# Gathering token rows in quarter pieces and transposing them on VectorE in a mixture-of-experts layer

## What is computed

```
idx, w = route(h2, w_router, bias)          # top 8 of 64 experts for every token
for each expert e:
    rows  = tokens that chose e
    y     = (silu(h2[rows] @ w_gate[e]) * (h2[rows] @ w_up[e])) @ w_down[e]
    acc[rows] += y * w[rows, e]
```

## Time and profile before

| | us |
|---|---|
| median of 3 runs (988.42 to 990.00) | 989.62 |
| span of the profiled execution | 986.4 |
| PE busy | 932.8 |
| DVE busy | 360.1 |
| ACT busy | 162.6 |
| POOL busy | 226.8 |
| data moved | 301.04 MB, mean 305 GB/s |

### The profile page before, as it was taken

How to read it: one execution, slowest core, us unless ns; L and a number is a source line. 1 busy time by engine, 2 the same in 40 slices (tenths; PEclk the granted TensorE clock), 3 DMA queues, 4 the chain that set the end, 5 groups by cost and what they waited for, 6 DMA issues and landing times.

```text
span 986.4 us, 15652 instructions
## 1 busy us (share of the span) xinstructions
PE 932.8 (95%) x6359; PEld 483.9 (49%) x6359; DVE 360.1 (37%) x773; ACT 162.6 (16%) x304; POOL 226.8 (23%) x344
## 2 busy tenths in 40 slices
PE   6999999999999999999999999989979889897798
PEld 4678788888655533333333333344323333332344
DVE  5565673336436733333332110111101111111687
ACT  2001324210011211111111111111101102121021
POOL 4115923162100112222222222212121211201110
PEclk9999999999999999999999999999989999999899
DMA  9940005421482699999999999999999999999972
GB/s 331 331 129 1 1 1 184 158 86 63 143 317 107 223 385 386 407 418 395 411 420 407 398 422 410 408 422 415 397 422 421 421 421 419 419 401 373 380 270 85
DMA packets 83912, 301.04 MB, mean 305 GB/s; under 512 B 9299, under 2 KB 35959, under 8 KB 59648
## 3 DMA queue, kind: packets, MB, share of 16 engines
q1 hardware_dynamic: 70144, 263.19, 67.8%
q0 software_dynamic: 11920, 33.63, 8.8%
q10 hardware_dynamic: 1776, 3.21, 0.9%
HBM read 279.26 MB, written 29.36 MB: 313 GB/s over the span
## 4 chain that ended last, share of the span: by engine, by line
PE 74%; DMA 20%; SPq 2%; DVE 2%; issue 1%; ACT 1%; POOL 0%; ACTq 0%; POOLq 0%
PE ps L2223 22%; DMA ring<-in_w_exp_up 18%; PE ps L1826 12%; PE ps L2252 8%; PE ps L1976 6%; PE ps L1955 5%; PE ps L2367 4%; PE ps L1782 3%; PE ps L1759 2%; PE ps L2047 1%; PE ps L1788 1%; DMA ring<-accumulator 1%; PE ps L2232 1%; DMA accumulator<-actT,stage 1%; SPq L525 1%; PE ps L1875 1%
## 5 line engine op out<-in xcount | busy, mean ns | idle before, releaser
L2223 PE MATMUL ps<-ring,gates 128*32 128x512 f32 x2560 | 289.3, 604 | 26.1 <-DMA ring<-in_w_exp_up 25.3
L2223 PEld LDWEIGHTS ps<-ring,gates 128*32 128x32 f32 x2560 | 88.8, 111 | 218.6 <-issue 217.7
L2252 PE MATMUL ps<-ring,poolbuf 128*32 128x512 f32 x1280 | 145.6, 595 | 3.1 <-DMA ring<-in_w_exp_down 3.1
L1573 DVE COPY poolbuf<-ps 128x256 f32<-128x256 f32 x40 | 17.0, 424 | 355.4 <-PE ps L2232 355.4
L791 POOL TENSOR_TENSOR tickets<-cst 128x1 f32<-128x1 f32 x77 | 14.5, 188 | 397.1 <-ACT actT L991 391.7
L2252 PEld LDWEIGHTS ps<-ring,poolbuf 128*32 128x32 f32 x1280 | 37.9, 109 | 83.5 <-issue 81.9
L991 ACT ACTIVATE actT<-ps,qT 128x1024 f32<-128x1024 f32 x40 | 44.5, 1113 | 142.3 <-PE ps L2252 142.3
L983 ACT ACTIVATE poolbuf<-ps 128x256 f32<-128x256 f32 x40 | 15.4, 384 | 280.0 <-PE ps L2223 280.0
L1826 PE MATMUL ps<-xrow,ring 128*128 128x256 f32 x256 | 57.9, 381 | 0.1
L1976 PE MATMUL ps<-ring,gates 128*128 128x512 f32 x128 | 56.4, 594 | 0.0
L1759 PE MATMUL ps<-cst,rows 128*128 128x128 f32 x352 | 47.6, 281 | 8.3 <-DVE rows L1087 8.3
(11 more groups left out here) (294 smaller groups left out, 1062.3 us busy)
## 6 DMA issues: line engine op xcount, KB each, us to landing
ring<-in_w_exp_down SPq DMA_DIRECT2D x64, 1024.0 KB, 17.6
ring<-in_w_exp_gate SPq DMA_DIRECT2D x62, 1024.0 KB
ring<-in_w_exp_up SPq DMA_DIRECT2D x62, 1024.0 KB
ring<-accumulator SPq DMA_DIRECT2D x12, 1024.0 KB, 13.1
ring<-in_w_gate SPq DMA_DIRECT2D x8, 1024.0 KB, 13.2
ring<-in_w_in SPq DMA_DIRECT2D x5, 1024.0 KB, 12.9
xrow<-in_x SPq DMA_DIRECT2D x8, 512.0 KB, 5.1
accumulator<-ring SPq DMA_DIRECT2D x1, 4096.0 KB, 19.9
```

Of the source, the lines that this page charges most:

```text
L2223: last = mm(bank(2 + k)[part, :], hgT[k][:, q, part], pair_view(EXPERT_SLOT[js[c]])[:, q], start=(q == 0), stop=(q == KD - 1))
L2252: last = mm(bank(6 + half)[part, :], eactT[r % 2][:, q, part], w[:, q, half * 512:(half + 1) * 512], start=(q == 0), stop=(q == 1))
```

## The change

The gathered rows come as quarters. `h2_dram` is seen as 2,048 rows of 256 numbers. One step has four gathers (c = 0 to 3), each of 128 pieces of 1 KB: partition 32q + n of columns 256c to 256c + 255 receives quarter q of the row in place 32c + n. With this layout, transposing each 32x32 block by itself gives the same `hgT` as before, so one VectorE operation (`block_T`) replaces eight TensorE transposes and two copies. Step 0 alone is still gathered in whole rows and transposed on TensorE.

For the pieces, VectorE makes `quarter_at`, four index columns per step, by 16 small operations per group (`quarters_of`). GpSimd reads the indices from there, without the stage copy. Lists are made in the steps of `LIST_STEP` = 0, 1, 2, 4, 5, 7, 8, 10, 12, 13, 15, 16, 18, 20, 21, 23 for groups 0 to 15, not in steps 0 to 15. `block_T(r+1)` stands first in VectorE's step r, ahead of `act_T(r-1)`, and waits for all four pieces.

```diff
+LIST_STEP = [0] + [1 + 22 * (g - 1) // 14 for g in range(1, NGROUP)]
...
+        h2_quarters = h2_dram.rearrange("t (q d) -> (t q) d", q=STRIPS)
...
+        def quarters_gathered(r):
+            return 64 * (r // BUF + 1) - (48 if r % BUF == 0 else 0)
...
-            def stage_from(r, j):
-                pool.wait_ge(rows_listed, STEP_OF[r][0] + 1)
-                nc.gpsimd.tensor_copy(stage[:, 0, j, :], from_row[:, r:r + 1]).then_inc(staged, 1)
...
-            def gather(j):
-                pool.indirect_dma_start(hg[j], None, h2_dram,
-                                        bass.IndirectOffsetOnAxis(ap=stage[:, 0, j, :], axis=0),
-                                        bounds_check=T - 1, oob_is_err=False).then_inc(gathered[j], 16)
+            def gather(r, j):
+                for c in range(STRIPS):
+                    pool.indirect_dma_start(hg[j][:, c * 256:(c + 1) * 256], None, h2_quarters,
+                                            bass.IndirectOffsetOnAxis(ap=quarter_at[:, 4 * r + c:4 * r + c + 1], axis=0),
+                                            bounds_check=4 * T - 1, oob_is_err=False).then_inc(gathered[j], 16)
...
                 if not last:
-                    pool.wait_ge(hgT_ps, 2 * r + 2)
-                    stage_from(r + BUF, j)
+                    if r:
+                        pool.wait_ge(blocks_ready, r)
+                    else:
+                        pool.wait_ge(hgT_ps, 2)
+                    pool.wait_ge(rows_listed, STEP_OF[r + BUF][0] + 2)
...
+            def quarters_of(g):
+                n = steps_of(g)
+                r = slice(FIRST_STEP[g], FIRST_STEP[g] + n)
+                at = quarter_at[:, 4 * FIRST_STEP[g]:4 * (FIRST_STEP[g] + n)].rearrange("p (s c) -> p s c", c=STRIPS)
+                for q in range(STRIPS):
+                    for c in range(STRIPS):
+                        last = nc.vector.tensor_scalar(at[q * STRIP:(q + 1) * STRIP, :, c],
+                                                       row_of[c * STRIP:(c + 1) * STRIP, r], float(STRIPS), float(q),
+                                                       ALU.mult, ALU.add)
+                last.then_inc(rows_listed, 1)
...
+            def block_T(r):
+                j = r % BUF
+                dve.wait_ge(gathered[j], quarters_gathered(r))
+                if r >= 2:
+                    dve.wait_ge(gu_ps, STRIPS * (r - 1))
+                nc.vector.transpose(hgT[r % 2].rearrange("p k (c n) -> p k c n", c=STRIPS),
+                                    hg[j].rearrange("p (c d k) -> p k c d", c=STRIPS, k=KD)).then_inc(blocks_ready, 1)
...
             for r in range(STEPS):
...
+                if r + 1 < STEPS:
+                    block_T(r + 1)
                 if r:
                     act_T(r - 1, (r - 1) % 2)
                 act_rows(r, r % 2)
-                if r + 1 < STEPS:
-                    rows_T(r + 1, (r + 1) % 2)
-                if 1 <= r < NGROUP:
+                if r in LIST_STEP[1:]:
...
                 up(r)
                 if r:
                     acts_T(r - 1)
-                if r + 1 < STEPS:
-                    rows_T(r + 1)
-                if 1 <= r < NGROUP:
-                    lists(r)
+                if r in LIST_STEP[1:]:
+                    lists(LIST_STEP.index(r))
```

More of the change, by code:

```diff
@@ L257, in build @@
         selb = ka[:, WM:WM + NR // 2].bitcast(BF16)
+        quarter_at = ka[:, 800:800 + 4 * STEPS].bitcast(U32)
         tokc = ka[:, WM + NR // 2:WM + NR // 2 + NT * TCOL // 2].bitcast(BF16).rearrange("p (i c) -> p i c", i=NT)
@@ L815, in move @@
                 if not last:
-                    pool.wait_ge(hgT_ps, 2 * r + 2)
-                    stage_from(r + BUF, j)
+                    if r:
[3 more added lines that the diff above has]
+                    pool.wait_ge(rows_listed, STEP_OF[r + BUF][0] + 2)
                     if not first:
                         pool.wait_ge(ticket_done[0], r)
-                    pool.wait_ge(staged, 2 * r + BUF + 1)
                     ticket(0, ticket_done[0])
-                    gather(j)
+                    gather(r + BUF, j)
                 if before is not None:
@@ L827, in move @@
                     pool.wait_ge(ticket_done[1], r)
-                pool.wait_ge(staged, STEPS + r + 1 if last else 2 * r + BUF + 2)
+                pool.wait_ge(staged, r + 1)
                 pool.wait_ge(y_ready, r + 1)
@@ L834, in _ @@
             pool.wait_ge(y_first, 16)
-            for r in range(BUF):
-                stage_from(r, r)
-                pool.wait_ge(staged, r + 1)
-                gather(r)
+            gather_first()
+            pool.wait_ge(rows_listed, 2)
+            for r in range(1, BUF):
+                gather(r, r)
             for r in range(STEPS):
@@ L1009, in _ @@
             nc.scalar.activation(hgT[0][:, 0:4, :], bank(0).rearrange("p (k n) -> p k n", k=4),
-                                 ACT.Copy).then_inc(hgT_lo_ready, 1)
-            rows_hi(0, 0)
+                                 ACT.Copy).then_inc(first_T_ready, 1)
+            act.wait_ge(hgT_ps, 2)
+            nc.scalar.activation(hgT[0][:, 4:8, :], bank(1).rearrange("p (k n) -> p k n", k=4),
+                                 ACT.Copy).then_inc(first_T_ready, 1)
             shared_silu_of(1)
@@ L1454, in rows_of @@
                 link(nc.vector.tensor_scalar(tile_of, found[:, :, 1], float(T), None, ALU.add))
-                nc.vector.tensor_tensor(from_row[:, r], tile_of, found[:, :, 0], ALU.add).then_inc(rows_listed, 1)
+                if g == 0:
+                    nc.vector.tensor_tensor(from_row[:, r], tile_of, found[:, :, 0], ALU.add).then_inc(rows_listed, 1)
                 link(nc.vector.tensor_tensor(row_of[:, r], tile_of, found[:, :, 0], ALU.add))
+            def quarters_of(g):
[8 more added lines that the diff above has]
+                last.then_inc(rows_listed, 1)
             dve.wait_ge(list_ps, 1)
@@ L1606, in _ @@
                 act_rows(r, r % 2)
-                if r + 1 < STEPS:
-                    rows_T(r + 1, (r + 1) % 2)
-                if 1 <= r < NGROUP:
-                    dve.wait_ge(list_ps, r + 1)
-                    rows_of(r, found_of(r))
-                    if r == 1:
+                if r in LIST_STEP[1:]:
+                    g = LIST_STEP.index(r)
+                    dve.wait_ge(list_ps, g + 1)
+                    rows_of(g, found_of(g))
+                    quarters_of(g)
+                    if g == 1:
                         weights_of(0, found_of(0))
-                    weights_of(r, found_of(r))
-                    if r + 1 < NGROUP:
-                        places(r + 1, rank3[:, :, (r + 1) * GROUP:(r + 2) * GROUP])
+                    weights_of(g, found_of(g))
+                    if g + 1 < NGROUP:
+                        places(g + 1, rank3[:, :, (g + 1) * GROUP:(g + 2) * GROUP])
                 for n in jobs_of(r, 0) + jobs_of(r, 1):
@@ L2202, in up @@
                 k = r % 2
-                pe.wait_ge(hgT_lo_ready, r + 1)
-                pe.wait_ge(hgT_hi_ready, r + 1)
+                if r:
+                    pe.wait_ge(blocks_ready, r)
+                else:
+                    pe.wait_ge(first_T_ready, 2)
                 if r == 1:
```

33 lines of the change are left out of this document (12 added, 21 removed).

## The result

The changed kernel took 995.82 us (median of 4 runs, 993.34 to 996.07), the kernel before 989.81 us beside it (4 runs). The ratio is 1.0055, with a 95% interval from 1.0041 to 1.0070: 4 to 7 us slower. The profiled execution took 996.04 us, its span is 994.2 us against 986.4.

The account below looks back on a forecast made before the run. The prediction took the DMA engines to bound the expert loop, with at most 4% free in the first half. Span 986.4 + 10.5 + 3 - 0.3 = 999.6 us, plus 3.2 for the timed run: 1002.8 us, range 995 to 1010.

Parts of the forecast that it names:

- Part 1: TensorE loses eight transposes in 39 steps: at most 16 us of PE time, worth 0.3 us at the very end.
- rival A: No slower, chance 0.16: pieces hidden beside 8 KB packets, TensorE's saved time counting in first half, 982.6 to 985.6 us.
- Part 2: Pieces on the DMA engines: 16,848 more q0 packets, 7.7 us for data pieces and 2.8 for empty packets, together 10.5.
- a share above 10%: Sign of a right forecast: q0 with about 28,768 packets and more than 10% share.
- Part 5: quarter_at and the lists, at the loop's start: gather(3) waits for group 1's list, +3 us (0 to 8).
- some 36 turns on engines that have loads: At the loop's start, gather(3)'s pieces wait behind loads on the DMA engines and land near 378 us.
- Part 3: GpSimd issues four gathers, not one: 3.1 to 4.7 us more per step, hidden; last piece 3 to 5 us later.
- Part 4: Block transpose on VectorE: 1.2 us taken, bounds 0.5 to 2.4; late pieces would delay the copy behind it and down(r-1).
- rival B: Chance 0.22: queue turns make pieces land late and set the step, 13.2 us against 12.15 in the first half, 1022 us.
- The spare of 5 us: Before the change, gathered rows landed at 464.7 us and were wanted at 469.8; the change was to use this up.
- rival B's signs: TensorE idle ahead of L2252 for the copy behind the block transpose; DMA share under 0.97 in the first half.
- The tail: After the last exp_up load lands, the last transposes stand on the path once: gain 0.3 us, 0.9 as other end.

Follow-up runs that it names:

- the runs with pauses: Three small linked GpSimd operations between issues in the second half, added to the kernel before with three empty gathers (1.0082) and with quarter pieces (1.0086).

## Why the prediction was right in sign and twice too large

**What bounds the kernel, and Part 1: right.** The DMA engines bound the loop in both halves. With the gather of whole rows back, 312 transposes fewer on TensorE gave a ratio of 1.0000, so rival A's gain in the first half (up to 7 us from "404 against 420 GB/s") doesn't exist: that gap is not free DMA time. The first wait for a weight load in the chain moved forward from 543 to 469 us; no other effect of the faster TensorE is seen. (Part 1's 16 us of TensorE time take 0.6 us for a step with lists, where its text has nearly 0.88; with 0.88 it would be 20. Neither number enters the sum.)

**Part 2, the main term: right place, wrong price.** That the four gathers cost time on the DMA engines, and that nothing hides it, is right. 10.5 us were summed; the last load landed 6.2 us later, and the pieces alone in the kernel before cost 7.1 (4.9 to 8.6 by the interval). The steps of its working that failed:

- The count. 28,768 packets were expected, 13,792 are there. The difference from before, 1,872, is 117 gathers with 16 closing packets each, so the data pieces added none: four pieces of 1 KB use as many packets as one row of 4 KB. The sign "a share above 10%" for q0 failed with it: it is 8.9%, where it was 8.8. The Trainium skill (DMA: Bandwidth & Descriptors, SWDGE vs HWDGE vs iDMA) has a packet of up to 4,096 bytes preferably and up to 64 descriptors; by this the trace agrees.
- The price of a piece with data. Weight loads with 1 KB packets at 350 GB/s gave 10 ns for each additional piece, above the cost of its bytes. But spread over all additional places, 3 x 128 x 40 = 15,360 on 16 engines, the 7.1 us are 7.4 ns each, and the 8.2 us of the empty gathers are 8.5 ns. Data or none makes no difference that can be seen. So what was priced as size is a price of places, and it isn't paid by q0's packets: q0 takes 0.9 us more in the two stretches above, and the loads on q1 take the rest. The 9 ns of an empty packet, from a line through two rates, is near these quotients by luck: it was used for 4,944 packets and not for 15,360 places, and with 128 more places in a step the same quotient is at most 5 ns. The rule of line rate from 512 bytes on (the Trainium skill, DMA: Bandwidth & Descriptors, Specifications) was held against the rows of 1 KB loads; for the pieces themselves it was nearer to what was measured than the forecast was, as no cost of their size is seen. What it leaves out is that places cost without any row in them.

**Part 5, the start: wrong, +3 forecast, about 0 measured.** The stretch has 379 GB/s against 373, so nothing was lost in it. The list of group 1 with its 16 operations ended at 361.9, and the four issues ran from 362.73 to 368.2, as expected. `up(3)` began at 378.13 us, 1.5 us later than 376.67. The prediction has two forecasts for this that don't agree: its working gives 379 (rows at 378, then the transpose), its sign 7 us after 376.7. The first is near, but by luck, since the wait that it rests on isn't there. `block_T` of step 3 began at 370.74, so all pieces had landed by then (start us, us, operation, idle before):

```profile
370.74 2.00 DVE L1592 STREAM_TRANSPOSE gates<-rows 128x1024 f32<-128x1024 f32 x1 [4.73 <-DMA rows<-h_rows,kT]
```
```profile
373.31 5.00 PE L2278 MATMUL ps<-ring,poolbuf 128*32 128x512 f32 x32 [3.18 <-DVE poolbuf L1602]
378.13 7.05 PE L2249 MATMUL ps<-ring,gates 128*32 128x512 f32 x64
```

The step that failed is "some 36 turns on engines that have loads": it put the landing at 378, 10 us behind the last issue, and it came at most 3.6 us after that issue began at 367.19. What held TensorE was the 3.2 us ahead of `down` for the copy behind `block_T`, and that isn't the pieces' doing: with one gather of whole rows it stood there as long, and its `up(3)` began at 378.48:

```profile
373.35 5.34 PE L2278 MATMUL ps<-ring,poolbuf 128*32 128x512 f32 x32 [3.59 <-DVE poolbuf L1602]
```

One step later the pieces are late, as the chain shows: the last one landed 10.5 us after its issue and 14.5 after the first of the four (370.66), where a gather of rows took 10.0.

```profile
374.65 10.50 DMA rows<-h_rows,kT
```

A start that loses DMA time exists, as the run with `block_T` behind `act_rows` shows (0.89, 332 GB/s, 4 us), but this change doesn't set it off.

**Part 3, GpSimd: right.** Four issues of 1.03 us stand in a step where one stood, POOL is busy for 343 us in place of 227, and the run with one gather and the runs with pauses show that none of it is on the path.

**Part 4: price wrong, conclusion right.** 2.05 us for `block_T`, inside 0.5 to 2.4 but not 1.2: it runs at half of an add's rate, as the upper end was built. The spare of 5 us is gone, as said: VectorE stands for the pieces and TensorE for the copy behind them (16.6 us). This is the first of rival B's signs. Its second, a DMA share under 0.97, isn't there. With one gather TensorE stands 15.1 us for the same copy, and the time is that of before; in the kernel before with pieces nothing waits behind a `block_T`, and the whole loss is there. So rival B has its wait and not its price. Its 36 turns for four pieces aren't there either: the count of packets leaves 8 with data and 4 closing ones for each engine.

**The tail: wrong by 1.9 us.** A gain of 0.3 was summed for the last transposes; 1.6 us were lost, by a last `up` at a granted clock of 0.81. The timed run lies 1.8 us above its span, and the forecast had added 3.2: that was the median over the span of one execution that was itself quicker than the median (executions of the kernel before take 1.8 to 1.9 us more than their span, so this one took some 988.3).

The whole miss of 7.0 us is then 7.3 (10.5 + 3 less 6.2, the main term and the start), less 1.9 in the tail, plus 1.4 between span and run, and 0.2 from that run to the median. These terms are read from one execution of each kernel; what the repeated runs carry is the 6.0 us in all and the 7.1 of the pieces.

## What to carry to other kernels

Where the DMA share is 1.00 through a loop, count what a change adds to the queues before what it saves on an engine, and read the GB/s beside the share, queue by queue: full and slower means that the same bytes take more of the engines' time, perhaps in another queue than the one that was changed. In an indirect DMA count the places, valid or not. To price them, add empty gathers to the kernel before, as many as the change will add, since one doesn't tell what three cost; this takes one run and says more than a rate borrowed from another queue's packets.

## What the runs showed of the hardware

- An indirect gather of 128 places that brings no row isn't free on saturated DMA engines: three more in each of 40 steps cost 8.2 us, two 5.8, one less than 1.3. The queue itself counts 32 packets for such a gather, with 16 places as with 128, so packets don't show this cost.
- With the pieces on q0, a megabyte of weights on q1 took 2.49 us of the 16 engines against 2.45, and 2.43 against 2.41 in the second half, while q0's own share rose by 0.2 and 0.3 points. Four pieces of 1 KB, from four gathers, add no packet with data to those of one row of 4 KB.
- Four gathers of 32 whole rows, each into a band of 32 partitions, cost 69 us more than one gather of the same rows into 128 partitions: 361 GB/s against 404, at a share of 1.02.
- A transpose of 32x32 blocks on VectorE over 128 x 1024 fp32 takes 2.05 us, 2 ns for an element of a partition, twice the 1.01 us of an add.
- TensorE stood idle for 2.65 us before the last `up`, which then ran at a mean clock of 0.81, 1.7 us longer than with 1.28 us idle and 1.00. In the two traces all 15 such products with 2.0 us of idle time or less ahead took 7.07 us, and 11 of the 13 with 2.6 us or more took 8.4 to 9.7. Whether the idle time is the cause wasn't tried.
